# A two-block transformer kernel on one core: ScalarE, in place of VectorE, multiplies the dilated heads' probabilities by the reciprocals of their sums

## The reference, cut to what matters

```python
DILATION_PATTERNS = ((128, 1), (512, 4), (2048, 16))

def dilated_window_branch(q, k, v, window, dilation, slopes):
    ...
    s = jnp.where(valid, s + bias, NEG_INF)
    lse = jax.nn.logsumexp(s, axis=-1)
    p = jnp.exp(s - lse[..., None])
    o = jnp.einsum('bhrnqk,bhrnkd->bhrnqd', p.astype(vc.dtype), vc)
    ...

def dilated_attention(q, k, v):
    ...
    w = jax.nn.softmax(jnp.stack(lses, axis=0), axis=0)
    o = jnp.stack(outs, axis=0).astype(jnp.float32)
    return jnp.sum(w[..., None] * o, axis=0).astype(q.dtype)
```

## Time and profile before

| | |
|---|---|
| median of 3 runs | 2445.4 us (2445.06 to 2454.4) |
| the profiled execution | 2445.81 us |
| its span, first to last instruction | 2443.6 us |
| TensorE matmul busy | 2408.1 us (99% of the span) |
| VectorE busy | 1781.7 us (73%) |
| ScalarE busy | 1185.1 us (48%) |
| GpSimd busy | 564.7 us (23%) |
| granted TensorE clock, mean | 0.997 |
| the dilated steps, their `soft` and `normal` | about 53 to 161 us of the span |

### The profile page before, as it was taken

The page is one execution under the profiler, slowest core; times in us unless marked ns, Lnnn a source line. Parts: engine busy times, 40 slices in busy tenths (PEclk is TensorE's granted clock), DMA queues, the critical chain, the costliest instruction groups (busy, mean ns, idle before and its releaser), DMA issues.

```text
span 2443.6 us, 35669 instructions
## 1 busy us (share of the span) xinstructions
PE 2408.1 (99%) x13533; PEld 2189.5 (90%) x13533; DVE 1781.7 (73%) x3391; ACT 1185.1 (48%) x2193; POOL 564.7 (23%) x372
## 2 busy tenths in 40 slices
PE   8999999999999999999999999999999999999998
PEld 7788888999999999999999998887888888888887
DVE  7876667998998886899999988777785336433323
ACT  6555466478778885333333345445322223332222
POOL 3222065133333541455555510000000000000000
PEclk9999999999999999999999999999999999999999
DMA  4111345699999999999999972222574322222331
GB/s 173 67 57 53 122 147 177 218 325 342 344 336 341 389 405 363 411 412 412 411 407 409 410 286 83 81 87 93 183 250 134 104 87 95 95 98 93 106 101 35
DMA packets 193114, 533.89 MB, mean 218 GB/s; under 512 B 16712, under 2 KB 65896, under 8 KB 190768
## 3 DMA queue, kind: packets, MB, share of 16 engines
q1 hardware_dynamic: 151472, 380.60, 43.3%
q0 software_dynamic: 41472, 151.01, 16.2%
HBM read 480.09 MB, written 51.46 MB: 218 GB/s over the span
## 4 chain that ended last, share of the span: by engine, by line
PE 91%; DVE 4%; ACT 2%; DMA 1%; issue 1%; DVEq 0%; SPq 0%; ACTq 0%
PE P L1351 28%; PE P L1353 28%; PE P L1352 28%; PE P L1716 2%; DMA hdram<-HID 1%; PE P L1358 1%; ACT wh L2539 1%; DVE wl L1826 1%; DVE T L1829 0%; PE P L1631 0%; PE P L1630 0%; PE P L1629 0%; PE P L1608 0%; PE P L1609 0%; PE P L1607 0%
## 5 line engine op out<-in xcount | busy, mean ns | idle before, releaser
L1351 PE MATMUL P<-XH,wh 128*128 128x512 f32 (+2 forms) x2272 | 833.9, 367 | 3.7 <-DVE wl L1826 3.7
L1353 PE MATMUL P<-XH,wl 128*128 128x512 f32 (+2 forms) x2272 | 817.6, 360 | 0.0
L1352 PE MATMUL P<-XL,wh 128*128 128x512 f32 (+2 forms) x2272 | 817.3, 360 | 0.0
L2539 ACT ACTIVATE wh<-raw 128x1024 fp32r<-128x1024 f32 x458 | 482.5, 1056 | 398.4 <-PE P L1353 398.4
L1826 DVE TENSOR_TENSOR wl<-raw,wh 128x1024 fp32r<-128x1024 f32 x422 | 512.6, 1223 | 84.5 <-ACT wh L2539 81.5
L1351 PEld LDWEIGHTS P<-XH,wh 128*128 128x128 f32 x2272 | 428.0, 188 | 48.2 <-DVE wl L1826 4.7
L1353 PEld LDWEIGHTS P<-XH,wl 128*128 128x128 f32 x2272 | 427.4, 188 | 47.6
L1352 PEld LDWEIGHTS P<-XL,wh 128*128 128x128 f32 x2272 | 428.2, 188 | 42.7 <-issue 1.9
L1351 PE MATMUL P<-AH,wh 128*128 128x368 f32 (+1 forms) x1024 | 337.4, 330 | 1.1 <-DVE AL L1826 1.1
L1352 PE MATMUL P<-AL,wh 128*128 128x368 f32 (+1 forms) x1024 | 336.7, 329 | 0.0
L1353 PE MATMUL P<-AH,wl 128*128 128x368 f32 (+1 forms) x1024 | 336.7, 329 | 0.0
(11 more groups left out here) (345 smaller groups left out, 3393.9 us busy)
## 6 DMA issues: line engine op xcount, KB each, us to landing
raw<-wts SPq DMA_DIRECT2D x211, 512.0 KB
raw<-ut SPq DMA_DIRECT2D x128, 512.0 KB
raw<-vt SPq DMA_DIRECT2D x128, 512.0 KB
hdram<-HID SPq DMA_DIRECT2D x64, 384.0 KB
HI<-hdram SPq DMA_DIRECT2D x32, 768.0 KB
gdram<-GS SPq DMA_DIRECT2D x23, 1024.0 KB
GI<-gdram SPq DMA_DIRECT2D x16, 1472.0 KB
AWC<-adat SPq DMA_DIRECT2D x64, 256.0 KB, 5.4
```

Source lines behind the costliest of these rows:

```text
L1351: e.matmul(bank, wh[:, w], H, start=start, stop=False)
L1352: e.matmul(bank, wh[:, w], L, start=False, stop=False)
L1353: return e.matmul(bank, wl[:, w], H, start=False, stop=stop)
L2539: return e.activation(dst, src, ACT.Copy)
```

## The change

Of the dilated steps (0 to 31) VectorE's `normal` ends after the reciprocal. The product with the reciprocal becomes an activation (Copy, with the reciprocal as scale for each row) on ScalarE, in a new function `normal` there, which waits for VectorE's reciprocal and raises `s_soft`. The fox steps (32 to 63) keep the product on VectorE; the first of them waits until `s_soft` shows that all 32 dilated steps are through.

```diff
+        divided = {}
...
                 step(e.reciprocal(st[:, c + 3:c + 4], st[:, c + 2:c + 3]).then_inc(s_v, 1))
+                divided[n] = step.n
+                if dilated(g):
+                    return
                 own()
+                v.wait_ge(s_soft, 32)
                 e.tensor_scalar(p_[:, 0:kw], p_[:, 0:kw], st[:, c + 3:c + 4], None, ALU.mult).then_inc(s_soft, 1)
...
+            def normal(n, g, h, qb):
+                if dilated(g):
+                    kw = 128 * (qb + 1)
+                    j = 4 * (n % 4)
+                    c.wait_ge(s_v, divided[n])
+                    e.activation(TB[n % 5][:, 0:kw], TB[n % 5][:, 0:kw], ACT.Copy,
+                                 scale=st[:, j + 3:j + 4]).then_inc(s_soft, 1)
```

More of the change, by code:

```diff
@@ L2915, in _ @@
             work = {f.__name__: f for f in (
-                high, gained, near, counts, square, root, gain, table, norm, forget, qk_split, v_copy, v_turn, soft, turn, values, subkeys, query, key,
-                token, gate, gate_turn, weigh, grid, hidden, rows, extra_turn, dots_end, mod_load, mod_part, rotation, square2, both_gains,
+                high, gained, near, counts, square, root, gain, table, norm, forget, qk_split, v_copy, v_turn, soft, normal, turn, values, subkeys, query,
+                key, token, gate, gate_turn, weigh, grid, hidden, rows, extra_turn, dots_end, mod_load, mod_part, rotation, square2, both_gains,
                 first_root, rope, r_copy, r_turn, r_decay, r_values, r_root, r_end, conv_c, conv_begin, conv, gate_a,
```

## The result

The changed kernel takes 2460.59 us (median of 6 runs, 2456.85 to 2461.58), the kernel before 2445.67 (6 runs). The ratio is 1.0054, with a 95% interval of 1.0042 to 1.0066: 14.9 us slower, three times the forecast's +5.0 and above the range's upper end of 2457.9. A later repeat (e9) gave 2461.25 against 2447.99, ratio 1.0057 (1.0040 to 1.0074). The time is nearest to the rival of the closed loop (2463.3).

What follows compares the result with a forecast made beforehand. TensorE was taken to bound the kernel, so only its waits for the softmax steps mattered. Longer turns of 13.0 us less 3.5, 1.95 and 2.55 gave +5.0: forecast 2450.4 us, range 2442.1 to 2457.9.

Steps and rivals of the forecast that it cites:

- the rival of the closed loop: VectorE and ScalarE alternate through every dilated turn, other work hides nothing: 17.9 us slower, 2463.3 us; chance 0.09.
- the value of the relief: Taking products off VectorE could win TensorE's 3.3 us of waits for products and PTL, 5.5 at most.
- the path: Reciprocal, product, copy to PTH and PTL come in line, lengthening a dilated turn by 0.59 us; 13.0 us after hiding.
- In 5 of 8 turns VectorE has other work ... I charge half there.: Work between reciprocal and PTL hides half the lengthening: 20 turns at 0.295 us, 12 at 0.59, together 13.0 us.
- The deductions: Taken off the 13.0 us of longer turns: 3.5 for idle time, 1.95 for collisions, 2.55 for distance to TensorE.
- The idle time ahead of `ML`: VectorE stands idle there for an output that TensorE sets; a late VectorE loses this first, minus 3.5 us.
- The collisions: Two VectorE products stretched by GpSimd's subtraction hold 3.9 us more; half was counted as gain, minus 1.95 us.
- The distance to TensorE: A product ends ahead of the transposes that need it, so 2.55 us of lateness are free once.
- all behind the stage moves alike: The dilated stage ends about 5 us later, and everything after it shifts by the same amount.
- The signs: Expected profile: PTL waits for PTH some 25 times, over 10 us; TensorE waits some 8; reciprocal waits a few tenths each.

Runs made afterwards that it cites:

- e9: The changed kernel unaltered, a plain repeat against the kernel before: 2461.25 us, ratio 1.0057.
- e2: Kernel before, product still on VectorE, with only ScalarE's wait for the reciprocal added where the changed kernel has its product: 2449.16 us, ratio 1.0006.
- e6: Changed kernel with VectorE's PTL moved from the start of its turn to behind the reciprocal, in all 64 steps: 2466.59 us, ratio 1.0081.
- e8: Changed kernel with ScalarE's product behind the copy to PTH (first two at once) and VectorE's PTL behind the reciprocal: 2465.76 us, ratio 1.0079.
- e4: Kernel before without any product in the 32 dilated steps, their probabilities left unnormalised: 2444.70 us, ratio 0.9988.
- e1: Changed kernel with ScalarE's product moved behind the copies MH and PTH of the same turn: 2454.09 us, ratio 1.0025.
- e3: Changed kernel with ScalarE's product covering one column instead of 128 to 512, same wait and order: 2452.28 us, ratio 1.0017.
- e5: Changed kernel with ScalarE's product behind the copy to PTH, but the products of steps 0 and 1 issued at once: 2449.41 us, ratio 1.0007.
- e7: Kernel before with VectorE's PTL moved behind the reciprocal and its product, in all 64 steps: 2468.17 us, ratio 1.0081.
- e10: The change made only for the narrow dilated steps (128 and 256 keys), against the kernel before: 2450.65 us, ratio 1.0014.
- e12: Changed kernel with a copy of the tile onto itself added ahead of ScalarE's product: 2474.62 us, ratio 1.0112 against the kernel before.
- e11: The change made only for the wide dilated steps (384 and 512 keys), against the kernel before: 2455.87 us, ratio 1.0036.

## Why the prediction was wrong

- **What bounds the kernel, the value of the relief, the direction.** Right. 3.3 us could be won by the waits; the kernel without any product is 2.5 us faster. The line reciprocal, product, copy, `PTL` is there and costs time, as the path said.
- **Durations.** Right to a few per cent. 0.53 forecast for the product, 0.56 measured. From the reciprocal to `PTL` a turn without other work became 0.53 us longer, 0.59 forecast.
- **"In 5 of 8 turns VectorE has other work ... I charge half there."** This step failed. By the timeline of the kernel before, 12 of the 32 turns have other work between reciprocal and `PTL`, not 20. And it hid next to nothing: these turns became 0.51 us longer, those without other work 0.53, where the forecast had 0.295 and 0.59. The other work waits for ScalarE as well. One such turn before, and after:

```profile
120.40 0.16 DVE L1983 RECIPROCAL st<-st 128x1 f32<-128x1 f32 x1
120.60 0.42 DVE L1985 TENSOR_SCALAR T<-T,st 128x384 f32<-128x384 f32 x1
121.05 0.69 DVE L1826 TENSOR_TENSOR ML<-P,MH 64x512 fp32r<-64x512 f32 x1
121.77 0.42 DVE L1826 TENSOR_TENSOR PTL<-P,PTH 128x256 fp32r<-128x256 f32 x1
```

```profile
126.86 0.16 DVE L1985 RECIPROCAL st<-st 128x1 f32<-128x1 f32 x1
128.32 0.69 DVE L1828 TENSOR_TENSOR ML<-P,MH 64x512 fp32r<-64x512 f32 x1 [1.30 <-ACT MH L2545]
129.05 0.42 DVE L1828 TENSOR_TENSOR PTL<-P,PTH 128x256 fp32r<-128x256 f32 x1
```

- **The deductions.** The idle time ahead of `ML` was to be lost first, 3.5 us. It grew instead, to 7.3 us in the waits listed above, although ScalarE's own waits there for TensorE, 3.1 us, fell to 0.2. The forecast's path with this deduction is 13.0 - 3.5 = 9.5 us; the timeline has 0.52 us in each of 31 turns, 16.1 us. The collisions were undercounted: the two turns whose product had met GpSimd became 0.94 and 1.48 us shorter, 3.5 us better than the others, where 1.95 was forecast. VectorE's products with the counts are stretched by GpSimd as much as before: added up over the timeline, 11.7 us over their usual times (0.29, 0.42, 0.56 and 0.69 us by width) before and 11.8 after. The Trainium skill, "SBUF — State Buffer", on who interferes with whom, says that ScalarE never waits for another engine there. The trace agrees as far as it goes: the 32 products on ScalarE take 0.39 to 0.72 us, and the three that ran beside a subtraction of GpSimd took 0.50, 0.41 and 0.52 us, as others of their widths. The distance to TensorE, 2.55 us in the forecast, gave at most 0.6: 16.1 - 3.5 = 12.6 us on VectorE, and the attention stage ended 12.0 us later.
- **The rival of the closed loop.** It had the right idea, that the other work hides nothing and that the idle time ahead of `ML` isn't given back, at a chance of 0.09. Its number, 17.9 us more, is near the measured 14.9 partly by luck: in the stage that it speaks of, 12.0 us were lost.
- **The rest of the time.** That all behind the stage moves alike was not quite so. Matmul by matmul, TensorE is 12.0 us late from the stage's end to about 800 us of the span and 15.7 from 980 us on: 3.7 us more are lost in between. From the stage's last matmul to the span's end it is about 2178.5 us in some profiles (before, e2, e6, e8; 2179.3 in e4) and 2181.9 to 2183.0 in others (the change, e1, e3, e5, e7, e9, e10, e12), with 2180.7 in e11. Part of it are TensorE's waits for ScalarE's `OM` in the experts' stage, 2.6 us before and 5.3 after. It goes with no edit: e6 and e7 fall on different sides. What decides it wasn't tried. With 12.0 us for the stage the forecast would have been 2457.4, at the range's upper end and 3 us under the measured time.
- **The signs.** Long waits for `PTH` and a new wait of TensorE for ScalarE's product came as said, the sums larger (20.1 us in 19 waits and 12.0 us, in place of "over 10" in "some 25" and "some 8"). ScalarE's waits for the reciprocal were longer than "a few tenths": 15 of them, 0.85 on average, the longest 2.1.

The general error: I found the line of dependence and then paid it out at a discount, from idle times and from other work, without asking of each discount which engine it waits for, and without counting in the timeline how many turns it holds for.

## What to carry to other kernels

The share of busy time told that VectorE was full and ScalarE had room; both were true and neither set the time of this stage. When work moves between two engines that each run in a fixed order, write down one turn of both queues and look for instructions that come to stand between a result of the one engine and that engine's next instruction. Put the moved work behind what the other engine waits for: the same products, one place later in ScalarE's queue, cost 2.5 us instead of 13 to 15. And ask first what the relief can bring at most; here it was 2.5 us of 2445.

## What was new of the hardware

On ScalarE a `Copy` from local memory to local memory takes 0.31, 0.42, 0.52 and 0.63 us for 128 to 512 columns, and with a scale for each row 0.40, 0.51, 0.62 and 0.72, so the scale costs 0.09 us at each of the four widths. Both ran in e12. Its copies are listed above (line 2684), and these are its products of 512 and 128 columns:

```profile
L2686 ACT ACTIVATE T<-T,st 128x512 f32<-128x512 f32 x8 | 5.8, 722 | 0.3
L2686 ACT ACTIVATE T<-T,st 128x128 f32<-128x128 f32 x8 | 3.2, 402 | 0.3
```

One column with a scale takes 0.29 us (e3): of the 0.56 us of the average product half doesn't depend on the width. The estimate from the exponentials with their per-row bias (0.37 to 0.69) was 0.03 us short at each width. They carry an operand of the same kind, which may be why it held; no run tested that.
